# Hybrid decoder layer: the search of block 7 and the scores of block 8 inside the projection, and attention's searches dealt gap by gap

## What is computed

```python
h = layer_norm(x, ln_in_g, ln_in_b)
proj = einsum('bld,de->ble', h, w_in)             # 256 + 768 + 256 + 256 + 512 + 64 + 8 columns
# pooling input, q (6 heads), k and v (2 heads), iq (8 x 64), ik (64), iw (8); rotary on q, k, iq, ik
def block(qb, iqb, iwb, q_pos):                   # 16 blocks of 128 queries
    s = einsum('bqhd,bsd->bqhs', iqb, ik)
    idx_score = einsum('bqhs,bqh->bqs', relu(s), iwb * w_scale)
    idx_score = where(causal, idx_score, NEG_INF)
    _, sel = top_k(idx_score, 256)                # the 256 best keys of each query
    ...                                           # softmax attention over the selected keys
mix = concat([pool_out, attn_out]) @ w_out
h = layer_norm(ALPHA_RES * h + mix, ln1_g, ln1_b)
# top-4-of-32 mixture of experts with clamped SwiGLU, and a last layer_norm
```

## Time and profile before

| | us |
|---|---|
| median of 3 runs | 4710.19 |
| lowest, highest | 4708.51, 4710.79 |
| the profiled execution | 4710.05 |
| its span in the profile | 4708.1 |
| TensorE busy (share of the span) | 4350.5 (92%) |
| VectorE busy | 3098.5 (66%) |
| ScalarE busy | 1816.1 (39%) |
| GpSimd busy | 933.7 (20%) |

### The profile page before, as it was taken

One profiled execution on the slowest core, in us unless ns is written; L12 is line 12 of the kernel. 1 busy time (PEld: TensorE's weight loads), 2 busy tenths in 40 slices (PEclk: granted clock), 3 DMA queues, 4 the chain that ended last, 5 costly groups with the idle time before them and its releaser, 6 DMA issues. The chain is left out here.

```text
span 4708.1 us, 69036 instructions
## 1 busy us (share of the span) xinstructions
PE 4350.5 (92%) x24163; PEld 3164.7 (67%) x24163; DVE 3098.5 (66%) x4884; ACT 1816.1 (39%) x2677; POOL 933.7 (20%) x1126
## 2 busy tenths in 40 slices
PE   8999978899988887399999999999999999999987
PEld 4444434444444443299998988989899998998961
DVE  2567747887778885245555655657566776776767
ACT  1222233343433333133334444444444555555530
POOL 0000012121111112211111212212122222222235
PEclk9999989999999998699999999999999999999996
DMA  5444230011010000344445536455466566666668
GB/s 187 119 121 123 66 93 24 21 25 19 15 28 15 15 13 14 97 148 165 156 136 208 191 138 228 170 200 201 174 224 217 208 231 229 213 232 225 217 219 335
DMA packets 525084, 666.35 MB, mean 142 GB/s; under 512 B 59201, under 2 KB 389441, under 8 KB 524897
## 3 DMA queue, kind: packets, MB, share of 16 engines
q1 hardware_dynamic: 400368, 484.87, 31.1%
q10 hardware_dynamic: 97984, 93.93, 6.1%
q0 software_dynamic: 26576, 85.56, 4.7%
HBM read 543.93 MB, written 120.36 MB: 141 GB/s over the span
## 5 line engine op out<-in xcount | busy, mean ns | idle before, releaser
L1956 DVE TENSOR_TENSOR w_lo<-w_raw,w_hi 128x2048 fp32r<-128x2048 f32 x386 | 874.5, 2286 | 557.7 <-ACT w_hi L2040 557.7
L1864 PE MATMUL gu<-x_hi,w_hi 128*128 128x240 f32 (+8 forms) x4096 | 1196.1, 292 | 21.5 <-DVE up L1971 15.7
L1867 PE MATMUL gu<-x_lo,w_hi 128*128 128x240 f32 (+8 forms) x4096 | 1192.6, 291 | 0.0
L1868 PE MATMUL gu<-x_hi,w_lo 128*128 128x240 f32 (+8 forms) x4096 | 1190.9, 291 | 0.0
L2040 ACT ACTIVATE w_hi<-w_raw 128x2048 fp32r<-128x2048 f32 x386 | 726.2, 1905 | 260.8 <-issue 144.5
L1864 PEld LDWEIGHTS gu<-x_hi,w_hi 128*128 128x128 f32 x4096 | 771.9, 188 | 25.8 <-DVE up L1971 18.9
L1868 PEld LDWEIGHTS gu<-x_hi,w_lo 128*128 128x128 f32 x4096 | 772.6, 189 | 0.0
L1867 PEld LDWEIGHTS gu<-x_lo,w_hi 128*128 128x128 f32 x4096 | 772.4, 189 | 0.2
L1838 POOL TENSOR_TENSOR a_lo<-up,a_hi 128x384 fp32r<-128x384 f32 x256 | 396.6, 1549 | 1213.6 <-ACT a_hi L2052 1213.6
L533 PE MATMUL proj_acc<-w_in_sb,hT 128*128 128x512 f32 (+1 forms) x1280 | 495.9, 535 | 0.7 <-ACT hT L549 0.7
L1864 PE MATMUL yp<-w_hi,a_hi 128*128 128x512 f32 x1088 | 445.4, 409 | 2.7
(11 more groups left out here) (299 smaller groups left out, 5734.4 us busy)
## 6 DMA issues: line engine op xcount, KB each, us to landing
w_raw<-w_gate_up SPq DMA_DIRECT2D x258, 1024.0 KB, 7.1
w_raw<-w_down SPq DMA_DIRECT2D x128, 1024.0 KB, 6.8
y_dram<-y_rows ACTq DMA_DIRECT2D x128, 256.0 KB, 2.2
y_dram<-zeros ACTq DMA_DIRECT2D x12, 2688.0 KB, 14.6
h_blk<-h_dram SPq DMA_DIRECT2D x32, 512.0 KB, 8.4
y_dram<-y_rows ACTq DMA_DIRECT2D x128, 128.0 KB, 6.5
qi_dram<-qi_stage ACTq DMA_DIRECT2D x16, 640.0 KB, 3.2
x_in<-x SPq DMA_DIRECT2D x16, 512.0 KB, 6.2
```

The costliest lines, as they stand in the source:

```text
L1864: op = nc.tensor.matmul(out, s_hi_, m_hi, start=(n == 0), stop=False)
L1867: nc.tensor.matmul(out, s_hi_, m_lo, start=False, stop=False)
L1868: op = nc.tensor.matmul(out, s_lo_, m_hi, start=False, stop=(n == len(pairs) - 1))
L1956: nc.vector.tensor_tensor(w_lo[:, c % 2, cols], raw[:, c % 3, cols], w_hi[:, c % 2, cols].bitcast(F32), ALU.subtract).then_inc(s_lo, 1)
```

## The change

- `EARLY` goes from 7 to 8: the projection searches blocks 2, 3, 4, 5, 7 and 6, in this order, and scores block 8; attention searches 8 to 15.
- `SLICE` goes from 25000 to 30000 (ns of search per tile).
- Gain and bias of the first norm, but for tile 0, move from VectorE to POOL (`affine`), behind a new semaphore `s_scaled`; POOL now signals `s_h`.
- The two score buffers and the two mask buffers of the projection get unequal sizes (`scores_of`, `mask_of`).
- Attention's phases are replaced by a fixed `ORDER` and by `plan`, which keeps an estimate of TensorE's and VectorE's time over all steps, hosts the scoring as early as it may, and gives VectorE bits in a step only while its estimate is not ahead of the next logits; what is left of a search in the last step ahead of its block is put there in full. A selection can come after any step.

```diff
-EARLY = 7
+EARLY = 8
...
-    SEARCHED = tuple(range(TOPK // P, EARLY))
+    SEARCHED = tuple(range(TOPK // P, EARLY - 2)) + (EARLY - 1, EARLY - 2)
...
-    SLICE = 25000
+    SLICE = 30000
...
+                def affine(t):
+                    row = x_in[:, t % 2]
+                    if t == 1:
+                        pool.wait_ge(s_const, 64)
+                    pool.wait_ge(s_scaled, t)
+                    nc.gpsimd.tensor_tensor(row, row, gain[:], ALU.mult)
+                    pool.drain()
+                    nc.gpsimd.tensor_tensor(row, row, bias[:], ALU.add).then_inc(s_h, 1)
...
                 for t in range(TILES):
                     if t + 1 < TILES:
                         power(t + 1)
+                        affine(t + 1)
...
-                    nc.vector.tensor_scalar(x_in[:, slot], x_in[:, slot], mean_var[:, 0:1], rstd,
-                                            ALU.subtract, ALU.mult)
+                    op = nc.vector.tensor_scalar(x_in[:, slot], x_in[:, slot], mean_var[:, 0:1], rstd,
+                                                 ALU.subtract, ALU.mult)
+                    if t:
+                        op.then_inc(s_scaled, 1)
+                        return
...
-    PHASES = ((0, 1, 2), (3, 7), (4, 15), (5, 14), (6, 13), (12,), (11,), (10,), (9,), (8,))
-    SEARCHED = tuple(b for blocks in PHASES for b in blocks if b >= EARLY)
+    ORDER = (1, 0, 3, 8, 4, 14, 5, 13, 7, 12, 15, 6, 11, 10, 2, 9)
+    SEARCHED = tuple(b for b in ORDER if b >= EARLY)
...
+    def plan():
...
+        for n, (k, i) in enumerate(gaps):
+            b = ORDER[k]
+            if i == 0 and b >= EARLY:
+                own = SEARCHED.index(b)
+                if s <= own:
+                    assert s == own and scored[s] < n - 1
+                    vector += sum(cost(s, x) for x in range(bit, BITS + 1))
+                    take(gaps[n - 1], s, bit, BITS + 1)
+                    chosen[s], chosen_at[s] = n - 1, vector
+                    s, bit = s + 1, 0
+                tensor = max(tensor, chosen_at[own])
...
+            while s < N_SEARCH and scored.get(s, n) < n and (s < 2 or free.get(SEARCHED[s - 2], n) < n):
+                if not bit:
+                    vector = max(vector, done)
+                if vector + cost(s, bit) * 0.6 > tensor + logits:
+                    break
+                vector += cost(s, bit)
+                take((k, i), s, bit, bit + 1)
+                bit += 1
+                if bit > BITS:
+                    chosen[s], chosen_at[s] = n, vector
+                    s, bit = s + 1, 0
...
                 def exp(k, i):
                     n = HEADS * k + i
                     if n == 0:
-                        for stored in S["qi_stored"]:
+                        for stored in (*S["qi_stored"], *S["iw_stored"]):
                             act.wait_ge(stored, 8 * TILES)
```

More of the change, by code:

```diff
@@ L186, in project_stage, with scores_of, mask_of @@
         bit_value, bit_next, same_row = S["bit_value"], S["bit_next"], S["same_row"]
-        scores = S["scores"][:].rearrange("p (s n) -> p s n", s=2)
-        mask = sb("mask_e", [P, 2, EARLY * P], BF16)
+        masks = sb("mask_e", [P, (2 * EARLY - 1) * P], BF16)
+        assert all(n <= (EARLY - s % 2) * P for s, n in enumerate(s_keys[:-1])) and 2 * EARLY * P == SEQ
+        def scores_of(s):
+            at = s % 2 * (EARLY + 1) * P
+            return S["scores"][:, at:at + s_keys[s]]
+        def mask_of(s):
+            at = s % 2 * EARLY * P
+            return masks[:, at:at + s_keys[s]]
         causal = [sb(f"causal{b}_e", [P, (b + 1) * P], BF16) for b in range(TOPK // P)]
@@ L311, in cut @@
                     pool.wait_ge(s_sc, chunk0[s + 1])
-                    tail = scores[:, s % 2, b * P:(b + 1) * P]
+                    tail = scores_of(s)[:, b * P:(b + 1) * P]
                     nc.gpsimd.affine_select(out=tail, in_=tail, compare_op=ALU.is_ge, fill=NEG, base=0,
@@ L429, in search @@
                         dve.drain()
-                    s, m = scores[:, n % 2, 0:s_keys[n]], mask[:, n % 2, 0:s_keys[n]]
+                    s, m = scores_of(n), mask_of(n)
                     for i in range(first, min(last, BITS)):
@@ L670, in attend_stage @@
     cut = [(b + 2) // 2 for b in ORDER]
[L672 to L692, removed]
     def values_part(k, g, part):
@@ L697, in values_part @@
         return range(cut[k]) if part == 0 else range(cut[k], ORDER[k] + 1)
[L699 to L726, removed]
@@ L730, in walk, with halved @@
+    def halved(k):
+        return keys[k] <= SEQ // 2
+    hosted, last_of, bits = plan()
     def walk(do):
@@ L749, in search @@
         def search(k, i):
-            if (k, i) in upto and "search" in do:
-                s, last, _ = upto[k, i]
-                before = [n for slot, (of, n, _) in upto.items() if of == s and slot < (k, i)]
-                do["search"](s, max(before, default=0), last)
-        def select(k):
-            if (k, HEADS - 1) in upto and upto[k, HEADS - 1][2] and "select" in do:
-                do["select"](upto[k, HEADS - 1][0])
+            if "search" in do:
+                for s, first, last in bits.get((k, i), ()):
+                    do["search"](s, first, min(last, BITS))
+                    if last > BITS:
+                        do["select"](s)
         for k in range(TILES + 2):
@@ L887, in attend_stage @@
         o_acc = ctx.enter_context(nc.psum_tensor("o_acc", [P, BANK], F32))
-        def halved(k):
-            return keys[k] <= SEQ // 2
         def qk_of(k, i):
@@ L969, in load_mask @@
                 def load_mask(k):
-                    users = [j for j in range(k) if loaded[j]]
-                    if users and keys[k] <= EARLY * P // 2:
-                        users = [j for j in users if j % 2 == k % 2]
+                    users = [j for j in range(k) if loaded[j] and (
+                        max(keys[j], keys[k]) > EARLY * P // 2 or j % 2 == k % 2)]
                     if users:
@@ L1014, in fetch, with apart @@
                     sp.dma_start(h[:], D_["h"][b * P:(b + 1) * P, :]).then_inc(s_hl, 16)
+                def apart(k):
+                    return not loaded[k] or max(keys[k], keys[k + 1]) <= EARLY * P // 2
                 def logits(k, i):
@@ L1019, in logits @@
                             load_q(k + 1)
-                            if loaded[k + 1] and (not loaded[k] or keys[k + 1] <= EARLY * P // 2):
+                            if loaded[k + 1] and apart(k):
                                 load_mask(k + 1)
@@ L1027, in late @@
                 def late(k):
-                    if k + 1 < TILES and loaded[k + 1] and loaded[k] and keys[k + 1] > EARLY * P // 2:
+                    if 0 < k and k + 1 < TILES and loaded[k + 1] and not apart(k):
                         load_mask(k + 1)
```

64 lines of the change are left out of this document (56 added, 8 removed).

## The result

| | before | after |
|---|---|---|
| median, us | 4709.35 (4 runs, 4702.45 to 4710.79) | 4748.24 (4 runs, 4741.15 to 4755.0) |
| the profiled execution, us | 4710.05 | 4751.97 |
| its span, us | 4708.1 | 4750.2 |
| first to last logits of attention, us | 1266.4 | 1226.4 |

After takes 1.0085 times as long (95% interval 1.0066 to 1.0105): 39 us slower, where I forecast 19. Read from the two profiles, the first logits begin at 695.64 for 613.79 (+81.9), attention from there to the last logits is 40.0 shorter, and the rest of the program is longer by 0.2. That gives the 42.1 by which the spans differ. The projection's sum came out near its forecast of 79; attention gave back 40 where I had 59.

The account below looks back on a forecast made before the run. TensorE was taken to bound the projection, with VectorE just about as fast, and to idle 171 us in attention, mostly on masks and turned probabilities. 4710 + 79 (projection) - 59 (attention) = 4730, stated as 4729 us; range 4698 to 4755.

Parts of the forecast that it names:

- Projection, +79 forecast: Projection: scores, rotation waits, late query loads and half-speed work together lengthen it by 79 us, between +60 and +85.
- Scores of block 8: Projection: scoring block 8 there adds 20.8 us, all on TensorE, which has nothing idle.
- Rotation waits: Projection, tiles 6, 8, 10, 12, 14: VectorE comes late, TensorE waits 1.9 us each for the rotated tile, +10 us.
- Query load: Projection: load behind SP's wait for h comes late; +28.8 us in tiles 6, 8, 10, 12, +13.5 in tile 14.
- Half-speed behind waits: Projection: after each of five long load waits TensorE works at half the granted clock, +7.5 us.
- Attention, -59 forecast: Attention: less idle time (-32), fewer half-speed stretches (-10) and block 8's scores gone (-17): -59 us, between -33 and -80.
- the other 108 us of idle time: Attention: TensorE's idle time besides mask waits shrinks to 44 us, with 30 and 70 as ends.
- The masks: Attention: search work left in last gaps makes TensorE wait 95 us for masks, against 63 before.
- (b): Projection: quick loads of 3.3 to 4.3 us and half the blocking; near 4706 us, no change; chance 0.20.
- (a): Projection: query loads stay hidden because blocking is cheap and VectorE keeps up; near 4688 us, faster; chance 0.15.
- (d): Attention: searches run later than planned, eight more bits in last gaps, no gain in small stalls; near 4769 us; chance 0.10.
- (e): Projection: block 7's selection isn't done in tile 13, block 6's lengthens projection by up to 5 us; 4734 us; chance 0.05.

Follow-up runs that it names:

- experiment 5: The kernel after, with the query load issued before SP's wait for h and uneven search slices (34 us in scoring tiles, 26 in others): 4691.49 us, ratio to before 0.9964.
- experiment 1: The kernel after, with SP issuing the query load before its wait for the next tile's h instead of behind it: 4709.64 us, ratio to before 0.9998.
- Experiment 6: The kernel after with the query load ahead of h, and attention's searches dealt by phases as in the kernel before: 4706.6 us, ratio to before 0.9999.
- experiment 10: The kernel after with early query load, uneven slices, a new order of attention's blocks and one scoring step at a place: 4650.48 us, ratio to before 0.9876.
- 11: The kernel after with early query load, uneven slices, a new order of attention's blocks and two scoring steps at a place: 4670.28 us, ratio to before 0.9912.
- experiment 2: The kernel after, with gain and bias back on VectorE in every tile and slices of 30 us kept: 4732.02 us, ratio to before 1.0045.
- experiment 3: The kernel after, with one step of block 14's scoring at each place of attention's first three blocks instead of two: 4745.01 us, ratio to before 1.0069.

## Why the prediction was right and wrong

**Projection, +79 forecast, +82 measured.** *Scores of block 8*, 20.8: first logits of experiment 5, with both kinds of wait gone, are 19.9 later than before's. *Rotation waits*, 10: 10.2, and 2.1 of TensorE's busy time that I had not given them. *Query load*, 28.8 + 13.5 = 42.3: 36.8. In tiles 6, 10 and 12 it was 7.2 as worked out. Tile 8's was 3.86, since its load was issued at 332.90, ahead of the zeros (334.15), and needed 5.5 us. Tile 14's was 11.24 for 13.5, since that load needed 3.4 us, not 5.2. *Half-speed behind waits*, 7.5: 11.8 behind the load's alone. Two misses of about 5 us cancelled, so that the sum came within 3 us is partly luck. That the order on SP's queue is the cause is shown by experiment 1; that VectorE's late round causes the other is shown by experiment 5; GpSimd's blocking was mis-sized by 10%.

**Attention, -59 forecast, -40 measured** (31 to 41 by the profiles with the same attention). This is the step that failed: "Of the other 108 us of idle time ... I keep 44". The masks were right to 2 us, 93.2 for 95, each block's within 1 us; so was the way to them, what the order leaves in the last gap. But the other idle time stayed at 71. I took the total of the waits for turned probabilities as mostly long stalls behind selections. Their long ones did go, and 36 short ones of 1 us stayed, 40 us with those of the output accumulator. And I priced no wait for scoring steps put two to a place, which were 18 us for 5. TensorE's busy time fell by 34, where scores and half-speed had 27; idle time by 6.5, where I had 32: a miss of 25 on idle time, less 7 on busy time that nothing here explains, is the 19 us. Experiment 6 shows more: the plan with this order of blocks was worth nothing beside an even spread, so what the prediction should have asked of the plan was whether it beats one, not which of its stalls go. Experiments 10 and 11 show that the same plan is worth something in another order.

Two of the sums don't come out: with 30 for the other idle time attention would be at -73, not at the -80 given as the lower end, and six half-speed stretches of 1.5 us are 9, not 10. Neither changes the account.

**The rivals.** (b) needed loads of 3.3 to 4.3 us, and in tiles 6 to 12 they took 5.5 to 7.2. (a) needed loads that stay hidden; experiment 1 makes this condition by hand and gave 4710, not 4688, since attention's -59 was missing there too (-34 in its profile). (d) had one mechanism that didn't happen, no extra bits slid into the last gaps; its other half, "no gain in small stalls", did in part: other idle time fell from 108 to 71, not to 44. (e) did not occur. The measured time lies above the forecast's own range (4714 to 4745) and inside the whole one, on the side of (d): for the small stalls.

## What to carry to other kernels

Before work is added to a stage that is full, look at what each queue issues behind a wait for the very engine that gets slower: here one load behind a store cost 37 us of waits and 12 of clock, and moving two lines took it back. A slice of filler work should be sized by the tile it runs in, not by the mean. When a table shows many short waits and a few long ones, forecast them apart: here the long ones went with their cause, and the short ones stayed. A schedule that replaces another should first be compared with an even spread of the same work, and tried in more than one order.

## What the hardware showed that I had not expected

The same load of queries ended TensorE's wait 7.2 us after its issue when it was issued 0.9 us behind a write of 2.7 MB by another queue, 5.5 when 1.3 us ahead of it (tile 8 of after), 3.6 when 1.5 ahead (tile 10 of experiment 2) and 3.4 with no such write (tile 14). So a shift of 2.4 us in the order of issue went with 3.6 us of landing time. It is not a rule of distance alone: 3.1 us ahead of the write it took 4.3 (tile 8 of experiment 2). Waits of 37 us in five places cost 11.8 us more of TensorE's time at a lower granted clock, and the first 155 us of attention ran at a clock of 0.81 to 0.83 with the change's order and two steps at a place, at 0.87 with one step (experiment 3) and at 0.90 in experiment 10, where TensorE is busy for 121, 129 and 130 us of them.
